# Encoder block with attention, gated linear attention and a mixture of experts: the first block's tokens come by a one-hot product on TensorE instead of a gather from memory, and the first scaling and last sums are reordered

## Chip, cores, metric

One core of one Trainium2 chip. The number told is device microseconds of one execution, the median over runs. The engines are named as the profile names them: PE is TensorE's matmul, PEld its weight load, DVE is VectorE, ACT is ScalarE, POOL is GpSimd, SP is SyncE, whose queue issues most transfers. An engine's name with a q (SPq, POOLq) is its issuing queue.

## What is computed

512 tokens of width 1024, all float32, one layer:

```python
n = rmsnorm(x, norm1_g);  proj = n @ w_in                      # 3104 columns
a = dilated attention(8 heads, 3 branches, relative bias)      # width 512
g = bidirectional gated linear attention(4 heads)              # width 512
x = x + concat([a, g]) @ w_out
h = rmsnorm(x, norm2_g)
logits = h @ router_w + router_b;  top 4 of 32 experts, softmax over the 4
for each block of one expert's tokens:
    hh = h[tokens] @ w1[e] + b1[e]                             # 1024 -> 2048, float32
    act = min(hh[::2], 7) * sigmoid(1.702 * ...) * (clip(hh[1::2], -7, 7) + 1)
    y += gate * (act @ w2[e] + b2[e])                          # 1024 -> 1024
out = rmsnorm(x + y, final_g)
```

## The kernel before

It is written by hand, engine by engine, with semaphores. Three stages follow one another.

**First stage, 0 to 277 us.** SP loads x in four tiles of 128 tokens and then the projection's weights, 2 MB at a time (L409 to L426). For each tile ACT squares and sums (L1057), DVE turns the sum into a mean plus epsilon (`inv_root`, L1260), ACT takes the root (`root`, L1046), DVE inverts it (L1262) and scales the tile (L1267), PE turns it (L554), and DVE or ACT copy it out of PSUM with the norm's weight (`turned_n`, L1271, and L1066). `pre_jobs` (L94) names every filling of a PSUM bank, in order, with the engine that empties it: of the halves of the turned tiles only (2, 1) and (3, 1) are ACT's. When all are out, PE runs the projections (L561, L568) and the two mixers.

**Second stage, 277 to 367 us.** PE multiplies by w_out (`mixed`, L734), half a tile at a time, and between these come, for the tile before, the turning of x (L743), the router's logits (L748), the ranks of the tokens within their experts (`ranks`, L756 and L757) and the table of who sits in which slot (`table`, L767). DVE adds the residual (L1457), picks the four experts (`top4`), turns ranks into one-hot rows (`slotted`, L1491 to L1499) and writes the entries of tokens that do not fit into an expert's 96 slots (`overflowing`). POOL and ACT make the normalised rows HN, and SP stores them to `hn_d` (L457). For the last tile nothing lies between: logits, `top4`, ranks, `slotted`, the total count, the table, its copy T96, its spreading over the partitions (`rep`, L820), and the copies into TABI and TAB (L1545, L1546). Then POOL gathers the first block's 96 rows out of `hn_d` (`gather`, L957) and DVE turns them into XT (`next_tokens`, L1552), in which feature 8p + k lies on partition p. Ahead of `next_tokens` stands DVE's computation of the block maps (L1573 to L1625): which experts have more than 64 tokens, in which order the blocks come, and how many there are. The counts (PAIRS, L1595 to L1599) say how often the loops run; PE, ACT, SP and POOL read them into registers with `value_load`.

**Third stage, from 367 us.** One block of 96 slots (3 groups of 32) after another, 32 experts: PE does `hidden` (L827: W1, 8 MB an expert) and `product` (L834: W2, 4 MB). `expert(i, q, groups)` works on all three groups or, in the second expert of the later pairs, on two. There are two W1 buffers and one for W2; SP reloads a piece when PE has signalled its use (`s_used`, `reload`, L483). The first pieces are loaded in the second stage: `static_w2` at once when the space of w_out is free, the last two of W1's second buffer (L464 and L467) later, since they lie on the router's operands; the first of these waits until the first gather is in (L463).

```python
        for f in range(2):
            static_w2(f, 0)

        sp.wait_ge(s_gath, 16 * NG)
        static_w1(1, 3, 1)
        wait_empty(sp, ("rep",))
        sp.wait_ge(s_pay, NT)
        static_w1(1, 2, 1)
```

Each block's result is added to `sum_d` by an indirect transfer (L1019). The last block's is not: SP loads the sums back (L520), POOL builds one-hot rows OHL (L1031), PE multiplies (L906) into four banks a tile, DVE adds four quarters a tile (`total`, L1697), ACT squares (L1235), and DVE scales (`final_norm`, L1690).

## Time and profile before

| | |
|---|---|
| median of 3 runs | 1380.0 us (1379.21 to 1380.11) |
| the profiled execution | 1385.87 us, span 1384.1 us |
| PE busy | 1266.7 us (92%) |
| DVE / ACT / POOL busy | 537.1 / 221.0 / 338.5 us |
| moved by DMA | 454.15 MB, mean 328 GB/s |
| mean granted TensorE clock | 0.970 of full speed |

The page's times are those of the profiled execution. A busy PE is one with a matmul under way, at whatever clock. Times below are microseconds from the start of the span, nanoseconds where marked.

### The profile page before, as it was taken

The numbers are of one execution on the slowest core, as the hardware profiler recorded it, in microseconds if no ns is written. First come the engines' busy times: TensorE is split into PE (matmuls) and PEld (weight loads), VectorE is DVE, ScalarE is ACT, GpSimd is POOL, SyncE is SP. The second block draws the span as 40 slices with busy tenths as digits, with TensorE's granted clock in tenths as the row PEclk, the third lists the DMA queues.
The fourth block names the chain that finished last, engine by engine and source line by source line (L and its number), as shares of the span: only waits on it lengthen the run. The fifth ranks groups of instructions, "written<-read, shape, count | busy, mean of one in ns | idle before, by whom it ended". The sixth has DMA issues, their size and how long they took to land.

```text
span 1384.1 us, 30020 instructions
## 1 busy us (share of the span) xinstructions
PE 1266.7 (92%) x12121; PEld 650.9 (47%) x12121; DVE 537.1 (39%) x1387; ACT 221.0 (16%) x446; POOL 338.5 (24%) x477
## 2 busy tenths in 40 slices
PE   6999999999599999999998987989898989899995
PEld 3444455655256676454344534343444434346532
DVE  2052353524433333344333444333333333345336
ACT  3052243423100000011000000000100000001102
POOL 2000000013522222223432222232333222222341
PEclk9999999999699999999999999999999999999998
DMA  9310000491799999999999999999999999999995
GB/s 327 114 63 2 27 27 1 161 381 62 304 384 413 410 404 393 401 402 418 414 416 412 413 419 417 417 417 415 415 418 413 413 414 413 416 377 418 394 414 187
DMA packets 62044, 454.15 MB, mean 328 GB/s; under 512 B 15119, under 2 KB 23911, under 8 KB 37436
## 3 DMA queue, kind: packets, MB, share of 16 engines
q1 hardware_dynamic: 40956, 432.18, 75.4%
q0 software_dynamic: 19184, 17.35, 5.7%
q10 hardware_dynamic: 1872, 4.18, 0.8%
q8 instruction: 22, 0.36, 0.1%
q14 instruction: 10, 0.08, 0.0%
HBM read 443.62 MB, written 18.65 MB: 334 GB/s over the span
## 4 chain that ended last, share of the span: by engine, by line
PE 56%; DMA 34%; DVE 3%; issue 2%; POOL 2%; ACT 1%; another core or an unknown queue 1%; POOLq 0%; SPq 0%; DVEq 0%
DMA mem<-in_w 28%; PE bank L827 17%; PE bank L834 16%; PE bank L568 6%; PE bank L561 6%; DMA sum_d<-mem 5%; PE bank L734 4%; PE bank L659 1%; PE bank L610 1%; POOL sum_d L1019 1%; PE bank L697 1%; PE bank L649 1%; POOL mem L957 1%; PE bank L704 1%
## 5 line engine op out<-in xcount | busy, mean ns | idle before, releaser
L827 PE MATMUL bank<-mem 128*32 128x512 f32 x5312 | 591.0, 594 | 14.0 <-DVE mem L1552 10.3
L827 PEld LDWEIGHTS bank<-mem 128*32 128x32 f32 x5312 | 259.9, 110 | 319.4 <-issue 267.3
L834 PE MATMUL bank<-mem 128*32 128x256 f32 x5312 | 339.8, 396 | 72.5 <-DMA mem<-in_w 58.3
L834 PEld LDWEIGHTS bank<-mem 128*32 128x32 f32 x5312 | 206.8, 114 | 202.8 <-DMA mem<-in_w 79.0
L1653 DVE TENSOR_TENSOR mem<-bank,mem 128x512 f32<-128x512 f32 x96 | 64.1, 668 | 412.7 <-PE bank L827 412.7
L1019 POOL DMA_INDIRECT sum_d<-mem x93 | 148.1, 1592 | 16.0 <-issue 16.0
L1221 ACT ACTIVATE mem<-mem 128x256 f32<-128x256 f32 x96 | 43.9, 457 | 607.0 <-DVE mem L1654 607.0
L1007 POOL COPY mem<-mem 128x3 f32 x31 | 6.4, 206 | 539.6 <-issue 539.6
L957 POOL DMA_INDIRECT mem<-hn_d,mem x99 | 103.0, 1040 | 31.8 <-issue 31.6
L1678 DVE TENSOR_TENSOR mem<-bank,mem 128x256 f32<-128x256 f32 x96 | 39.4, 421 | 183.8 <-PE bank L834 107.0
L1227 ACT ACTIVATE mem<-mem 128x256 f32<-128x256 f32 x96 | 47.0, 506 | 318.7 <-DVE mem L1678 258.5
L568 PE MATMUL bank<-mem 128*128 128x512 f32 x192 | 85.6, 599 | 0.0
L561 PE MATMUL bank<-mem 128*128 128x512 f32 x192 | 83.3, 594 | 1.5 <-ACT mem L1066 1.5
L966 POOL TENSOR_TENSOR mem<-mem 128x512 f32<-128x512 f32 x8 | 10.1, 1268 | 223.1 <-DVE mem L1457 223.1
L1663 DVE STREAM_TRANSPOSE mem<-mem 128x256 f32<-128x256 f32 x96 | 62.0, 646 | 3.3
L734 PE MATMUL bank<-mem 128*128 128x512 f32 x128 | 58.0, 598 | 1.2 <-ACT mem L1041 1.2
L561 PEld LDWEIGHTS bank<-mem 128*128 128x128 f32 x192 | 36.2, 190 | 47.9 <-issue 47.0
L568 PEld LDWEIGHTS bank<-mem 128*128 128x128 f32 x192 | 35.5, 190 | 46.7 <-issue 45.5
L933 POOL TENSOR_TENSOR mem<-mem 128x1 f32<-128x1 f32 x130 | 47.9, 368 | 38.5 <-ACT mem L1227 35.5
L1552 DVE STREAM_TRANSPOSE mem<-mem 128x256 f32<-128x256 f32 x99 | 55.3, 609 | 0.0
L1657 DVE SCALAR_TENSOR_TENSOR mem<-mem 128x256 f32<-128x256 f32 x96 | 42.0, 437 | 12.1
L1661 DVE TENSOR_TENSOR mem<-mem 128x256 f32<-128x256 f32 x96 | 41.3, 430 | 3.3
(249 smaller groups left out, 707.0 us busy)
## 6 DMA issues: line engine op xcount, KB each, us to landing
mem<-in_w SPq DMA_DIRECT2D x192, 2048.0 KB
mem<-in_w_in SPq DMA_DIRECT2D x6, 2048.0 KB, 13.1
mem<-in_w_out SPq DMA_DIRECT2D x1, 4096.0 KB, 15.2
mem<-rel_d ACTq DMA_DIRECT2D x8, 448.0 KB, 5.3
mem<-in_x SPq DMA_DIRECT2D x4, 512.0 KB, 5.3
hn_d<-mem SPq DMA_DIRECT2D x4, 512.0 KB, 15.6
sum_d<-mem SPq DMA_DIRECT2D x4, 512.0 KB
mem<-sum_d SPq DMA_DIRECT2D x4, 512.0 KB, 5.0
```

What stands on the lines that cost most here:

```text
L561: m = pe.matmul(b[:, :], w[:, k, c * P:(c + 1) * P], NTt[:, k, :], start=k == 0, stop=k == NK - 1)
L568: m = pe.matmul(b[:, :], NTt[:, k, t * P:(t + 1) * P], w[:, k, :], start=k == 0, stop=k == NK - 1)
L734: m = pe.matmul(b[:, :], MIX[:, k, t * P:(t + 1) * P], WO[:, k, n * 512:(n + 1) * 512], start=k == 0, stop=k == NK - 1)
L827: m = pe.matmul(bank[r][GR * j:GR * (j + 1), :], XT[:, r, k, :], W1[q][:, k, 512 * j:512 * (j + 1)], start=k == 0, stop=k == NK - 1)
L834: m = pe.matmul(bank[3 + r][GR * j:GR * (j + 1), 0:256], ATT[:, r, 2 * f2 + c, :], W2[:, 2 * f2 + c, 256 * j:256 * (j + 1)], start=f2 == 0 ...
L933: pool.tensor_tensor(held[:, 2 + n:3 + n], held[:, 0:1], held[:, 1:2], ALU.add)
L957: pool.indirect_dma_start(out=XG[:, r, :], out_offset=None, in_=quarters, in_offset=bass.IndirectOffsetOnAxis(GI[:, r:r + 1], 0), bounds_c ...
L1019: pool.indirect_dma_start(out=sum_d.ap(), out_offset=bass.IndirectOffsetOnAxis(SI[:, r:r + 1], 0), in_=YN[:, r, :], in_offset=None, bounds ...
L1227: act.activation(YN[:, r, :], YB[:, r, :], ACT.Copy, scale=GTC[:, r:r + 1]).then_inc(s_yn, 1)
L1552: v.transpose(XT[:, r, :, :], XG[:, r, :].rearrange("p (i k) -> p k i", k=NK)).then_inc(s_xt, 1)
L1653: step(v.tensor_tensor(z, bank[r][:, :], B1T, ALU.add))
L1663: v.transpose(ATT[:, r, :, :], ACTV[:, r, :].rearrange("p (i f) -> p f i", f=NF)).then_inc(s_at, 1)
```

## The change

It has five parts.

1. **First scaling.** ACT takes the root straight from its own sum, with epsilon and 1/1024 in the activation (`mean_root`); DVE's step goes. The half (1, 1) of the turned tiles goes from DVE to ACT. DVE's order becomes normalized 0, 1, turned (0,0), normalized 2, turned (0,1), normalized 3, turned (1,0), (2,0), (3,0).
2. **First block's tokens.** In `slotted`, three more DVE operations make OH0, a one-hot row per token with the token's inverse root in the column of its slot if its expert is expert 0. PE multiplies x of each tile (stationary, every eighth column) by OH0: four matmuls of 128x128 by 96 columns for each tile and half, 32 in all, accumulated in two banks. ACT copies them into XT with norm2's weight. The first gather and its turning go; the gather of the second block comes first.
3. **Block maps.** DVE computes the part that the counts need first, and the rest after TABI and TAB.
4. **Loads.** L464's load no longer waits for a gather. The one after it waits also for XT. One small load (G2K, 128 times 32 bytes) stands ahead of w_out's.
5. **Last sums and signals.** The last block's sums for tile 0 start in PSUM with x itself (identity matmuls) and are squared and scaled from there; tile 3 is added in one operation; the order of totals and scalings changes. In two-group experts the second group's signals come from its own last matmul, and the small extra matmul (`also`) signals the third's.

```diff
-    jobs += [(("nT", t, q), "a" if t >= 2 and q else "v") for t in range(NT) for q in range(2)]
+    jobs += [(("nT", t, q), "a" if t and q else "v") for t in range(NT) for q in range(2)]
...
+    OH0 = [view(at + 2 * COLS * (t % NG) + 2 * E + SLOTS * (t // NG), SLOTS) for t in range(NT)]
...
+    WIDE = banks[:, 1024:3072].rearrange("p (j n) -> p j n", j=NJ)[:, :, 0:D // NJ]
...
-    LAST = ((6, 7, 0, 1), (2, 3, 4, 5))
+    LAST = ((2, 3, 4, 5), (6, 7, 0, 1), (6, 7, 0, 1), (2, 3, 4, 5))
...
+        sp.dma_start(G2K, bass.AP(norm2_g.tensor, 0, [[NK, P], [1, NK]])).then_inc(s_g2k, 16)
         sp.dma_start(WO, w_out.rearrange("(k p) n -> p k n", p=P)).then_inc(s_wo, 16)
...
-        sp.wait_ge(s_gath, 16 * NG)
         static_w1(1, 3, 1)
+        sp.wait_ge(s_xt, NG)
         wait_empty(sp, ("rep",))
         sp.wait_ge(s_pay, NT)
         static_w1(1, 2, 1)
...
+        def first_tokens(t, h):
+            b = bank_of(("x0", h))
+            if t == 0:
+                begin(("x0", h))
+            pe.wait_ge(s_oh0, t + 1)
+            for c in range(4):
+                m = pe.matmul(b[:, c * SLOTS:(c + 1) * SLOTS], X[:, t, bass.ds(4 * h + c, P, NK)], OH0[t],
+                              start=t == 0 and c == 0, stop=t == NT - 1, skip_group_check=True)
+            return m
...
         full(("lg", u), logits(b, u, range(4, NK)))
+        first_tokens(0, 0)
+        first_tokens(0, 1)
+        first_tokens(1, 0)
         ranks(u)
...
         full(("total",), pe.matmul(b[:, 0:E], ones, MSEL[:, u, :], start=False, stop=True))
+        first_tokens(1, 1)
+        for t in range(2, u):
+            for h in range(2):
+                first_tokens(t, h)
+        for h in range(2):
+            full(("x0", h), first_tokens(u, h))
         full(("tab",), table(u))
...
-                if r < groups - 1:
+                if r < NG - 1:
                     m.then_inc(s_hf, 1)
             if groups < NG:
-                also().then_inc(s_hf, 1)
+                also().then_inc(s_used, 1)
...
+        pe.wait_ge(s_yl[0], 16)
+        for j in range(NJ):
+            if j:
+                pe.wait_ge(s_yb, 2 * NG * pairs + (NG + j))
+            pe.matmul(bank[LAST[0][j]][:, 0:D // NJ], ident, XF[:, 0, j * (D // NJ):(j + 1) * (D // NJ)],
+                      start=True, stop=False, skip_group_check=True)
...
-        gather(slice(0, 1), 3)
-        pool.wait_ge(s_xt, NG)
-        gather(slice(1, 2), 4)
+        gather(slice(1, 2), 3)
         overflow(3)
...
+        def mean_root(t, done):
+            act.wait_ge(s_sq, done)
+            act.activation(st4[:, t:t + 1], st4[:, t:t + 1], ACT.Sqrt, bias=EPSt, scale=1.0 / D).then_inc(s_sd, 1)
...
+        act.wait_ge(s_g2k, 16)
+        act.wait_ge(s_hst[NT - 2], 16)
+        act.wait_ge(s_hst[NT - 1], 16)
+        for h in range(2):
+            wait_full(act, ("x0", h))
+            for c in range(4):
+                k = 4 * h + c
+                ins = act.activation(XT[:, :, k, :], bank_of(("x0", h))[:, c * SLOTS:(c + 1) * SLOTS].rearrange(
+                    "p (r i) -> p r i", r=NG), ACT.Copy, scale=G2K[:, k:k + 1])
+            if h == 0:
+                emptied_by(ins)
+        ins.then_inc(s_xt, NG)
...
-            v.tensor_scalar(stat, stat, 1.0 / k, EPS, ALU.mult, ALU.add).then_inc(s_var, 1)
...
             link(v.tensor_reduce(RA[:, TOPK * t:TOPK * (t + 1)], OHV, AX.X, ALU.add))
+            link(v.scalar_tensor_tensor(FST, RA[:, TOPK * t:TOPK * (t + 1)], 1.0, OHT[t % 2][:, :, 0], ALU.add, ALU.mult))
+            link(v.tensor_reduce(RK, FST, AX.X, ALU.add))
+            v.tensor_scalar(OH0[t], CF[:, CIO + 1:CIO + 1 + SLOTS], RK, st4[:, t:t + 1],
+                            ALU.is_equal, ALU.mult).then_inc(s_oh0, 1)
...
-        next_tokens(1)
+        v.wait_ge(s_b1, 16)
+        next_b1()
...
         v.wait_ge(s_fg, 16)
-        total(0)
         total(1)
-        for t in range(NT):
+        final_norm(0)
+        total(2)
+        total(3)
+        for t in range(1, NT):
             final_norm(t)
-            if t + 2 < NT:
-                total(t + 2)
```

## Rows read from the trace of the kernel before

**Rows 1.** The page's part 4: share of the chain that ended last

```profile
PE 56%; DMA 34%; DVE 3%; issue 2%; POOL 2%; ACT 1%; another core or an unknown queue 1%; POOLq 0%; SPq 0%; DVEq 0%
```

**Rows 2.** Two experts by windows: length, busy PE to POOL, PEclk, DMA share, GB/s

```profile
402.00:435.00 33.00, 32.77 (x384) 21.75 (x382) 12.34 (x29) 2.92 (x7) 10.12 (x14) 1.00 1.02 411
785.00:817.00 32.00, 27.85 (x301) 11.73 (x297) 12.09 (x29) 2.85 (x6) 9.27 (x13) 0.95 1.02 415
```

**Rows 3.** Timeline of the start: start, length, engine, line, count, idle before, releaser

```profile
2.62 0.48 SPq L413 DMA_DIRECT2D mem<-in_w_in  x1
...
9.52 1.06 ACT L1057 ACTIVATE mem<-mem 128x1024 f32<-128x1024 f32 x1 [0.24 <-DMA mem<-in_x]
...
13.44 0.20 ACT L1046 ACTIVATE mem<-mem 128x1 f32<-128x1 f32 x1 [1.68 <-DVE mem L1260]
...
13.88 0.75 DVE L1267 TENSOR_SCALAR mem<-mem 128x1024 f32<-128x1024 f32 x1
...
14.55 1.88 DVE L1271 TENSOR_TENSOR mem<-bank,mem 128x512 f32<-128x512 f32 x3
...
15.87 1.14 ACT L1066 ACTIVATE mem<-bank,mem 128x128 f32<-128x128 f32 x4 [0.54 <-DVE mem L1271]
...
17.27 7.10 PE L561 MATMUL bank<-mem 128*128 128x512 f32 x16 [1.50 <-ACT mem L1066]
```

**Rows 4.** DMA issues between 2.5 and 2.7 us: count, KB, us to landing

```profile
mem<-in_w_in SPq DMA_DIRECT2D x1, 2048.0 KB, 12.9
```

**Rows 5.** Timeline of the second stage's end, PE, DVE and SP

```profile
347.05 1.31 PE L748 MATMUL bank<-mem 128*128 128x32 f32 x8 [0.94 <-DVE mem L1470]
350.16 0.64 PE L756 MATMUL bank<-mem 128*128 128x32 f32 x2 [1.80 <-DVE mem L1483]
353.31 1.54 PE L767 MATMUL bank<-mem 128*96 128x64 f32 x8 [1.23 <-DVE mem L1499]
...
356.98 0.25 DVE L1546 COPY mem<-bank 128x96 f32<-128x96 f32 x1
...
357.70 0.16 DVE L1512 SCALAR_TENSOR_TENSOR mem<-mem 128x4 f32<-128x4 f32 x1
...
364.61 0.80 SPq L437 DMA_DIRECT2D mem<-in_w  x2
...
367.03 10.61 PE L827 MATMUL bank<-mem 128*32 128x512 f32 x73 [10.27 <-DVE mem L1552]
...
378.03 13.43 SPq L474 DMA_DIRECT2D mem<-in_w  x4
```

**Rows 6.** Windows there, columns as in rows 2

```profile
348.00:350.00 2.00, 0.36 (x2) 0.22 (x2) 1.43 (x7) 1.79 (x3) 1.39 (x3) 0.50 0.46 178
371.00:373.00 2.00, 2.00 (x20) 0.56 (x16) 0.00 (x0) 0.00 (x0) 1.51 (x4) 0.84 1.04 442
362.50:365.00 2.50, 0.00 (x0) 0.00 (x0) 2.23 (x18) 0.00 (x0) 0.00 (x0) 0.50 0.27 95
376.50:379.00 2.50, 2.33 (x21) 0.82 (x19) 0.00 (x0) 0.00 (x0) 0.09 (x1) 1.00 0.12 27
```

**Rows 7.** Timeline: POOL after a register load, PE after a wait and without

```profile
396.90 0.19 POOL L949 TENSOR_TENSOR mem<-mem 128x3 int32<-128x3 int32 x1 [0.67 <-issue]
...
1357.67 5.35 PE L834 MATMUL bank<-mem 128*32 128x256 f32 x64 [2.10 <-DMA mem<-in_w]
```

**Rows 8.** One line each: four DVE sums, strided and not

```profile
L1483 DVE TENSOR_REDUCE mem<-mem x4: 369/372/374, 299.7 to 349.7; 128x32 f32<-128x128 f32 x4
...
L1494 DVE TENSOR_REDUCE mem<-mem x4: 286/286/286, 304.1 to 351.6; 128x4 f32<-128x128 f32 x4
```

**Rows 9.** Timeline of the end, PE and DVE

```profile
1368.16 2.01 PE L906 MATMUL bank<-mem 32*128 32x256 f32 x32 [0.90 <-POOL mem L1031]
1369.47 2.74 DVE L1697 TENSOR_TENSOR mem<-mem,bank 128x256 f32<-128x256 f32 x8 [0.86 <-PE bank L906]
...
1379.68 1.28 DVE L1690 SCALAR_TENSOR_TENSOR mem<-mem 128x1024 f32<-128x1024 f32 x1
```

More of the change, by code:

```diff
@@ L138, in pre_jobs @@
         late += [(("wo", t, 1), "v")]
-    late += [(("xT", NT - 1, 1), "v"), (("lg", NT - 1), "v"), (("rank", NT - 1), "v"), (("total",), "v")]
+    late += [(("xT", NT - 1, 1), "v"), (("lg", NT - 1), "v"), (("rank", NT - 1), "v"), (("total",), "v"),
+             (("x0", 0), "a"), (("x0", 1), "a")]
     for name, e in late:
@@ L220, in encoder_block @@
     JUNK2 = view(take(512), 512)
+    FST, RK, G2K = view(take(TOPK), TOPK), view(take(1), 1), view(take(NK), NK)
     assert at <= o_ks, at
@@ L314, in encoder_block @@
     thr = CF[:, CTH:CTH + THR].unsqueeze(1)
-    bank = [ctx.enter_context(nc.psum_tensor(f"bank{i}", [P, 512], F32)) for i in range(8)]
+    banks = ctx.enter_context(nc.psum_tensor("banks", [P, 8 * 512], F32))
+    bank = [banks[:, 512 * i:512 * (i + 1)] for i in range(8)]
+    WIDE = banks[:, 1024:3072].rearrange("p (j n) -> p j n", j=NJ)[:, :, 0:D // NJ]
     rel_d = nc.dram_tensor("rel_d", [HA, REL], F32)
@@ L905, in _ @@
                 for j in range(NJ):
-                    m = pe.matmul(bank[LAST[t % 2][j]][:, 0:D // NJ], OHL[GR * j:GR * (j + 1), r, t * P:(t + 1) * P],
-                                  YN[GR * j:GR * (j + 1), r, :], start=r == 0, stop=r == NG - 2)
+                    m = pe.matmul(bank[LAST[t][j]][:, 0:D // NJ], OHL[GR * j:GR * (j + 1), r, t * P:(t + 1) * P],
+                                  YN[GR * j:GR * (j + 1), r, :], start=t > 0 and r == 0, stop=r == NG - 2,
+                                  skip_group_check=True)
             m.then_inc(s_add, 1)
@@ L1012, in _ @@
             pool.wait_ge(s_xt, NG * g + 2 * NG)
-            gather(bass.ds(column, 1), g + 5)
+            gather(bass.ds(column, 1), g + 4)
             pool.wait_ge(s_si, g + 1)
@@ L1165, in _ @@
         turned(5, (0, 2))
-        root(NT + 1, st16)
+        root(1, st16)
         turned(6, (0, 2))
@@ L1199, in _ @@
             squares(t, 1)
-            root(NT + 2 + t, st4[:, t:t + 1], EPSt)
+            root(2 + t, st4[:, t:t + 1], EPSt)
             act.wait_ge(s_hx, 2 * t + 2)
@@ new lines, in _ @@
+        v.tensor_scalar(PAIRS[:, N_EARLY:N_EARLY + 1], FULL[0:1, :], float(rest), PNL[0:1, 0:1],
+                        ALU.is_equal, ALU.add).then_inc(s_emap, 1)
+        v.tensor_scalar(PAIRS[:, N_PAIRS:N_PAIRS + 1], FULL[0:1, :], float(rest), PNE[0:1, 0:1],
+                        ALU.is_equal, ALU.add).then_inc(s_emap, 1)
+        wait_full(v, ("rep",))
+        rows = bank_of(("rep",))[:, 0:NG * 2 * E].rearrange("p (g e v) -> p g e v", g=NG, v=2)
+        v.tensor_copy(TABI[:, :, 0:E, 0], rows[:, :, :, 0]).then_inc(s_tabr, 1)
@@ L1583, in _ @@
+        emptied_by(v.tensor_copy(TAB[:, :, 0:E, 1], rows[:, :, :, 1]))
+        overflowing(u)
+        linked(v.tensor_scalar(FULL2, FULL, 2.0, None, ALU.mult),
                v.tensor_scalar(FIRST, FULL, float(rest), None, ALU.add),
@@ L1667, in _ @@
                 swiglu(r)
-            next_tokens(g + 2)
+            v.wait_ge(s_b1, 16 * g + 32)
+            v.wait_ge(s_gath, 16 * NG * g + 16 * NG)
+            for r in range(NG):
+                v.transpose(XT[:, r, :, :], XG[:, r, :].rearrange("p (i k) -> p k i", k=NK)).then_inc(s_xt, 1)
+            next_b1()
             v.wait_ge(s_b2, 16 * g + 32)
```

113 lines of the change are left out of this document (51 added, 62 removed).

## Prediction, made before the changed kernel was run

> **What bounds the kernel now.** I read the chain that ended last first, since the shares of busy time mix three stages. PE holds 56% of it and DMA 34% [rows 1]; in order of time it is PE in the first half of the span and mostly weight loads in the second. The windows say more: already in the expert from 402 to 435 us PE is busy 32.8 of 33 us and the DMA engines are full at 411 GB/s, and in a later one PE has room (27.9 of 32) and the DMA is full at 415 GB/s [rows 2]. An expert's 12 MB of weights, with its tokens fetched and results added, take 32 to 33 us in both. So from the first reload at 378 us [rows 5] the kernel is one long stream of weights, and no part of the change makes the stream shorter. What can be won is its beginning, and the tail behind it. Three places matter: the start, before the first projection; 348 to 378 us, where PE has nothing to do for 10.27 us and the DMA is idle twice; and the last 16 us.
>
> **The start.** In the row of tile 3, ACT has the square done at 10.6 us, but its root starts at 13.44, after 1.68 us of waiting for DVE's step L1260, which stands behind other DVE work [rows 3]. With the root on ACT alone it is there at about 11.0 (10.58, and 0.2 each for reading the sum and for the root). Then DVE counts: when x of tile 3 lands at 9.5 it still has turned (0,0), normalized 2 and turned (0,1) ahead, 0.63 + 0.95 + 0.63 = 2.2 us (1.88/3 a copy; 0.75 and 0.2 for a scaling with its inverse), so that tile 3's scaling starts near 11.9 instead of 13.88. That is 2.0 us less, and PE's first projection would start at 17.27 - 2.0 = 15.3. ACT has one copy more (1.14 us), but ahead of tile 3's, in time that it waits. The next thing that is late is a load: w_in's first 2 MB are issued at 2.62 and land 12.9 us later, at 15.5 [rows 3, 4]. So PE starts at 15.6: **1.6 us** won, and it carries on, for all up to 348 us follows PE, ACT or DVE (bounds: 0.5, if ACT's copies come in its way, and 1.7). The G2K load ahead of w_out costs its issue, 0.48 us as L413's, and PE asks for w_out only after the mixers' last copies; I take 0, and 0.5 for the range. Three more DVE operations in `slotted` for tiles 0 to 2, about 0.2 us each by L1512, lie beside w_out's matmuls: 0.
>
> **The middle**, in times of the profile of before. Logits end at 348.4. PE then waits 1.8 us for ranks at 350.16 [rows 5]. In that gap the change puts 12 of the 32 products, 24 PE instructions (two a float32 matmul). No row has this shape. Nearest are the logits, 8 instructions in 1.31 us, and the ranks, 2 in 0.43 to 0.64, all with 128 columns of weights: 0.107 us at full clock to 0.215 at half. The granted clock is 0.50 at 348 to 350 us, that is 1.2 GHz, and PE had been stopping and starting for 3 us before it fell; after 367.03 it takes 4.6 us of unbroken work until 2.4 GHz is granted (0.84 over 371 to 373) [rows 6]. So the 24 run 4.7 us at half speed (22 of them) and end at 353.3. Ranks and total, 8 instructions, behind them: the rank is there at 353.9, and the total is out at 354.2. Before it was 351.2: the gap filler **costs 2.7 us**.
>
> DVE then does `slotted` with the new three: 2.0 us from rank (351.3) to table operands (353.3) becomes 2.6, to 356.5. PE meanwhile: 24 instructions for (1,1) and tile 2, to 356.8; 16 for tile 3, to 358.6; table, 8 at 0.08 to 0.1, to 359.3 (1.54 before, at half clock); T96 0.25; `rep`, 6, to 360.3; TABI and TAB, as at 356.8 to 357.2, to 360.9. The counts, now ahead of these on DVE, are in by 360.5. ACT's eight copies (0.28 each by L1066 [rows 3]) end 1.4 us after the last product, at 360.1: not last. Last are the two register loads that PE makes after `rep` is emptied and that 5 us of waiting hid before: POOL's load shows 0.67 us [rows 7], so 1.4. PE starts the first expert at **362.3 instead of 367.03: 4.7 us** earlier. Of what was there, the gather, its landing, its turning and DVE's block maps leave the path; the maps still end near 365 on DVE, but SP needs them only for the reload.
>
> The clock: after a wait of 2.1 us at 1355.6 PE took 5.35 us for 64 products of 256 columns, four side by side [rows 7], which at full speed are 16 times 0.22 = 3.5 (L561 takes 0.44 for 512 columns [rows 3]). The wait for the registers is 2 us long, so I take a fall again and 1.8 us lost. Before, 73 products of 512 columns took 10.6 us [rows 5] for 8.0 at full speed: 2.6 lost. That is 0.8 won, 5.5 in all, up to 7.3 if the clock holds.
>
> Against this stands the DMA. It can only be moved up by what it stood idle: 2.5 us at a share of 0.27 and 2.5 at 0.12, 1.8 + 2.2 = 4.0, with the edges about 4.9 [rows 6]. Both gaps go. L437's first load waited until 364.61 for the gather and now follows w2's at once; its second, at about 362, is issued while the first is under way, and together they last to 373; the first reload comes 11 us after PE's start (367.03 to 378.03), at 373.3. Smaller of 5.5 and 4.9: I take **4.8 us**. For POOL, the second block's gather comes ahead of overflow(3) as before, 7 us earlier; nobody waits for it before 387. SP's new wait for XT has only loads behind it and ends before `rep` is emptied.
>
> **The tail.** PE starts on OHL's last row at 1368.16 and DVE ends at 1380.96 [rows 9]; between them DVE does four totals (2.74/2 = 1.37 each) and four scalings (about 1.45), 11.3 us from 1369.47. After: three totals and four scalings, 9.9, from when PE has tiles 0 and 1, which is one identity matmul (0.43) later than before, 1370.7. End at 1380.6: **0.4 us**. Reading four banks at once is unseen here; between 0 and 1.2 us for the range. `also` shifts signals by 0.3 us, where the DMA is the bound: 0.
>
> **Sum.** 1.6 + 4.8 + 0.4 = 6.8 us. The working is made in a profiled execution of 1385.87 us (span 1384.1); I take the difference, not the time, over to the median: 1380.0 - 6.8 = **1373.2 us**.
>
> **A rule that speaks against it.** The stationary operand is every eighth column of x, a step of 32 bytes. The trace has such a step only on DVE: a sum of 128 elements read with a stride takes 0.372 us, without one 0.286 [rows 8]. I keep 0.107 us for PE, since PE's weight loads of 128 columns at either clock just follow the clock. The Trainium skill (SBUF — State Buffer, section "Door 1: The DMA port swizzle") says that full bandwidth needs two accesses to each 16-byte line, so four float32 are the largest free step. By that rule each of the 64 loads would be dearer; the factor is not given.
>
> **Rivals.**
> *Part of the middle is eaten (chance 0.20).* PE's code arrives cold at the loop, register loads take longer than POOL's, or the clock stays low through the 40 later products. For it: everything in 353 to 362 is a chain, and PE has no slack before the loop now. Against: no such stop shows at 277. Middle 1.5: 1376.5 us.
> *The start of the experts doesn't move (0.08).* Then only start and tail count: 1378.0. It would need XT or the counts at 367; nothing above adds up to it.
> *Strided weights cost twice (0.08).* 0.107 more on each of 64: PE is 2.6 us later at ranks and 6.8 later at its first expert, 369.1 instead of 362.3. Middle -2: 1.6 - 2.0 + 0.4 = 0, 1380.0 us. That is where the skill's rule leads, if "dearer" is double.
> *Strided weights cost three times (0.06).* The same place: 13.6 us on the path, 6.9 slower, 1386.9. From 2.4 times on it is slower than before by over 0.2%. For it speaks the DVE pair, which shows that strides are not free; against it that its factor is 1.3.
> *The forecast (0.58).* 1370.5 to 1375.5.
>
> **Chances and range.** A measurement of this kernel tells 0.2%, 2.8 us. Faster by more: forecast, and most of the first rival, 0.76. Within: 0.03 of that rival, the second, the third, 0.18. Slower: 0.06. The range takes the forecast's bounds, the first rival and most of the second: 1370.5 to 1378.3.
>
> **What would show it.** First projection at 15.6, right behind w_in's landing; if at 17, the start failed. PE's ranks at 353.3 less 1.6 with the clock at 0.5; if before 350.5, the filler was free. LDWEIGHTS of the new products as long as others of 128 columns, 0.1 to 0.2 us. First expert at 360.7 (362.3 less 1.6), waiting for a register or `rep`, not XT. No DMA gap between 350 and 380. Last scaling 11.4 us or so after OHL. I am wrong if a weight load in the new line takes 0.3 us, if PE waits for ACT's XT, or if the DMA falls idle elsewhere.

## The result, and the profile after

The changed kernel takes **1383.05 us** (median of 20 runs, 1381.3 to 1385.05) beside 1380.38 us for the kernel before. The ratio is 1.0019, 95% interval 1.0012 to 1.0025: about 2.7 us slower, just under what one measurement tells from no change. Predicted were 1373.2 us and 1370.5 to 1378.3; the prediction was wrong. The profiled execution took 1381.3 us, with a span of 1379.5.

The start did what it should. Timeline of the changed kernel from 10 to 16 us (start, length, engine, line, count, idle before, releaser):

```profile
11.62 0.75 DVE L1314 TENSOR_SCALAR mem<-mem 128x1024 f32<-128x1024 f32 x1
...
15.11 2.84 PE L570 MATMUL banks<-mem 128*128 128x512 f32 x6 [1.59 <-DMA mem<-in_w_in]
```

Tile 3's scaling (L1314) begins at 11.62 instead of 13.88 and the first projection at 15.11 instead of 17.27 [rows 3]; it now waits for w_in's landing and not for ACT. In this execution that is the predicted next thing.

The middle did not. PE's timeline from the last logits to the first expert:

```profile
345.58 1.08 PE L757 MATMUL banks<-mem 128*128 128x32 f32 x8 [0.95 <-DVE mem L1516]
346.50 6.02 PE L775 MATMUL banks<-mem 128*128 128x96 f32 x24
352.31 0.53 PE L765 MATMUL banks<-mem 128*128 128x32 f32 x2
...
353.94 9.81 PE L775 MATMUL banks<-mem 128*128 128x96 f32 x40
363.54 1.44 PE L787 MATMUL banks<-mem 128*96 128x64 f32 x8
365.38 1.51 PE L849 MATMUL banks<-mem 96*128 96x64 f32 x6 [0.41 <-DVE mem L1617]
369.22 11.35 PE L856 MATMUL banks<-mem 128*32 128x512 f32 x88 [2.32 <-issue]
```

L775 is the new product. Its 40 later instructions take 9.6 us, 0.24 us each, where I had 0.107 for an operand of neighbouring columns. The first expert starts at 369.22, later than the 367.03 of before [rows 5], although everything ahead of it came 1.5 us earlier (logits at 345.58 instead of 347.05). From the end of the logits to the first expert it is 22.6 us instead of 18.7. The idle time there is gone: PE is the bound of this stretch. The last wait, 2.32 us "issue", is where the program has PE's two register loads.

The weight load of that line, and for comparison one of the same shape from neighbouring columns (lines from 300 to 380 us, PEld: count, busy us, mean ns, idle before):

```profile
L775 PEld LDWEIGHTS banks<-mem 128*128 128x128 f32 x64 | 15.4, 335 | 0.0
L743 PEld LDWEIGHTS banks<-mem 128*128 128x128 f32 x76 | 13.6, 190 | 12.9 <-issue 12.9
```

335 ns is above the 0.3 us that I had named as the sign of being wrong; the weight loads overlap, so the cost is the spacing, 0.24 us.

Windows of the changed kernel (columns as in rows 2):

```profile
348.00:350.00 2.00, 2.00 (x10) 2.00 (x9) 0.89 (x4) 1.56 (x5) 1.53 (x2) 0.70 1.05 393
360.00:362.00 2.00, 2.00 (x10) 2.00 (x10) 0.00 (x0) 0.04 (x1) 0.00 (x0) 0.50 0.93 393
...
366.00:369.00 3.00, 0.90 (x5) 0.71 (x4) 1.89 (x15) 0.00 (x0) 1.32 (x3) 0.50 0.01 3
371.00:373.00 2.00, 2.00 (x16) 0.49 (x12) 1.76 (x16) 0.00 (x0) 1.82 (x3) 0.58 0.94 389
376.00:378.00 2.00, 2.00 (x24) 0.62 (x20) 0.00 (x0) 0.00 (x0) 0.98 (x1) 1.00 0.33 65
402.00:435.00 33.00, 33.00 (x408) 12.36 (x404) 12.77 (x33) 3.38 (x7) 11.18 (x16) 1.00 1.02 414
785.00:817.00 32.00, 25.52 (x280) 9.67 (x276) 11.72 (x29) 2.74 (x6) 9.26 (x13) 0.89 1.02 417
```

The two experts further on are as before [rows 2]: the stream of weights is as fast as it was. The DMA gap at 362 to 365 [rows 6] is closed, but two new ones are there, 366 to 369 and 376 to 378. And the granted clock falls while PE is busy, 0.70 over 348 to 350, and is at 0.50, 1.2 GHz, at 360 and up to the first expert, though from 346.5 to 366.9 PE stopped once, for 0.4 us; over 371 to 373 it is still 0.58.

SP's timeline names the loads behind the two gaps:

```profile
349.75 19.27 SPq L446 DMA_DIRECT2D mem<-in_w  x2
376.93 0.35 SPq L483 DMA_DIRECT2D mem<-in_w  x1
```

L446's first load (W1's last piece but one) is issued at 349.75, behind w2's, as the change wants. Its second is issued only at the end of that group, at 368.70, after a wait of 18.3 us. SP's waits, and ACT's copies of the second half of XT:

```profile
SPq L475 <- DVE mem L1566: 18.3, 1, 18.3
...
363.79 1.03 ACT L1254 ACTIVATE mem<-banks,mem 128x96 f32<-128x96 f32 x4 [0.79 <-PE banks L775]
```

The program has three waits there: XT (the new one), `rep` emptied, and `s_pay`. XT was complete at 364.82. L1566 is the last of DVE's entries of the last tile's tokens (`overflowing`), which signals `s_pay`; it stands behind TABI and TAB on DVE and ended at 368.60. So it is a wait that was there before, and it is late because the table is: the long products hold it up.

The first reload (L483) needs PE's first uses of the first expert, and comes at 376.93; before it was 378.03 [rows 5].

The tail, DVE's timeline:

```profile
1366.87 1.41 DVE L1758 TENSOR_TENSOR mem<-mem,banks 128x256 f32<-128x256 f32 x4 [2.88 <-PE banks L943]
...
1371.01 1.22 DVE L1754 TENSOR_TENSOR mem<-mem,banks 128x1024 f32<-128x1024 f32 x1
...
1375.13 1.28 DVE L1747 SCALAR_TENSOR_TENSOR mem<-mem 128x1024 f32<-128x1024 f32 x1
```

From PE's last L863, at 1358.95, to DVE's end at 1376.41 it is 17.46 us. Before, from L834's 1363.29 (of the same trace as rows 9) to 1380.96, it was 17.67. The tail won 0.2 us. The addition that reads four banks at once takes 1.22 us, where four separate ones take 1.41.

### The profile page after: what moved, and what is told of

It is laid out like the page before. It is cut to its first block, busy times and chain, and to the rows that moved or that the text cites. A ratio compares the mean times of both kernels' runs of the same rounds, so it can differ in the third digit from the quotient of the medians.

```text
span 1379.5 us, 30137 instructions
## 1 busy us (share of the span) xinstructions
PE 1257.6 (91%) x12193; PEld 542.7 (39%) x12193; DVE 532.2 (39%) x1384; ACT 223.4 (16%) x458; POOL 335.1 (24%) x472
## 4 chain that ended last, share of the span: by engine, by line
PE 58%; DMA 37%; DVE 3%; issue 1%; ACT 1%; SPq 0%; DVEq 0%
DMA mem<-in_w 37%; PE banks L863 17%; PE banks L856 16%; PE banks L577 6%; PE banks L570 6%; PE banks L743 4%; PE banks L775 1%; PE banks L668 1%; PE banks L619 1%; DMA mem<-in_w_in 1%; PE banks L706 1%; PE banks L658 1%; PE banks L713 1%; PE banks L757 0%; PE banks L641 0%
## 5 line engine op out<-in xcount | busy, mean ns | idle before, releaser
L856 PE MATMUL banks<-mem 128*32 128x512 f32 x5312 | 579.9, 595 | 5.9 <-DMA mem<-in_w 3.6
L863 PE MATMUL banks<-mem 128*32 128x256 f32 x5312 | 316.7, 398 | 91.3 <-DMA mem<-in_w 84.2
L856 PEld LDWEIGHTS banks<-mem 128*32 128x32 f32 x5312 | 169.3, 110 | 393.5 <-issue 384.5
L863 PEld LDWEIGHTS banks<-mem 128*32 128x32 f32 x5312 | 171.1, 115 | 238.2 <-DMA mem<-in_w 106.9
L1700 DVE TENSOR_TENSOR mem<-banks,mem 128x512 f32<-128x512 f32 x96 | 63.6, 663 | 411.6 <-PE banks L856 411.6
L1056 POOL DMA_INDIRECT sum_d<-mem x93 | 148.1, 1592 | 17.6 <-issue 17.6
L1731 DVE TENSOR_TENSOR mem<-banks,mem 128x256 f32<-128x256 f32 x96 | 39.4, 421 | 176.7 <-PE banks L863 176.7
L995 POOL DMA_INDIRECT mem<-hn_d,mem x96 | 99.9, 1041 | 31.1 <-issue 31.1
L577 PE MATMUL banks<-mem 128*128 128x512 f32 x192 | 85.6, 599 | 0.0
L570 PE MATMUL banks<-mem 128*128 128x512 f32 x192 | 83.4, 594 | 1.6 <-DMA mem<-in_w_in 1.6
L971 POOL TENSOR_TENSOR mem<-mem 128x1 f32<-128x1 f32 x129 | 50.9, 394 | 35.1 <-ACT mem L1279 31.9
L743 PE MATMUL banks<-mem 128*128 128x512 f32 x128 | 58.0, 598 | 1.2 <-ACT mem L1078 1.2
L570 PEld LDWEIGHTS banks<-mem 128*128 128x128 f32 x192 | 36.2, 190 | 48.0 <-issue 46.2
L577 PEld LDWEIGHTS banks<-mem 128*128 128x128 f32 x192 | 35.5, 190 | 46.7 <-issue 45.5
```

The source lines that it names most:

```text
L570: m = pe.matmul(b[:, :], w[:, k, c * P:(c + 1) * P], NTt[:, k, :], start=k == 0, stop=k == NK - 1)
L577: m = pe.matmul(b[:, :], NTt[:, k, t * P:(t + 1) * P], w[:, k, :], start=k == 0, stop=k == NK - 1)
L743: m = pe.matmul(b[:, :], MIX[:, k, t * P:(t + 1) * P], WO[:, k, n * 512:(n + 1) * 512], start=k == 0, stop=k == NK - 1)
L856: m = pe.matmul(bank[r][GR * j:GR * (j + 1), :], XT[:, r, k, :], W1[q][:, k, 512 * j:512 * (j + 1)], start=k == 0, stop=k == NK - 1)
L863: m = pe.matmul(bank[3 + r][GR * j:GR * (j + 1), 0:256], ATT[:, r, 2 * f2 + c, :], W2[:, 2 * f2 + c, 256 * j:256 * (j + 1)], start=f2 == 0 ...
L971: pool.tensor_tensor(held[:, 2 + n:3 + n], held[:, 0:1], held[:, 1:2], ALU.add)
```

## The experiments

**Theories.** S: the products' stationary operand is every eighth column, and its weight load costs 0.24 us instead of 0.107; this holds up PE and, through it, the last early load and the first reloads. Rivals: the two-group signals (part 5) let the loads of the later experts come late; the products ahead of the ranks are the cost and the rest is free; the start's gain was never there. The runs of one group below were made on one chip with the kernel before beside them; two_step, listed with the third, had a group of its own. The groups differ: in the result's, the second and the third the kernel before takes 1380.4 to 1380.5 us, in the first 1387.3 and in two_step's 1386.4. So only ratios are compared across groups.

### First group: the same kernel again, the start alone, two parts undone

**before_again**, no edit.

> The kernel before, unchanged, for a second profile. Its first profiled execution took 1385.87 us, 5.5 us above its median, and moved 394 to 411 GB/s between 432 and 592 us, where the changed one moved 410 to 418. If that was this one execution's own trouble, the new profile shows 413 or more there, a time near 1380.4 and a last weight wait that ends near 1358; then the changed kernel's stream is about 4 us longer than the typical one of before, and that needs a cause. If it is a trait of the kernel before, the rates repeat near 400.

Measured: ratio 1.0 (0.9991 to 1.001), profiled execution 1384.2 us. The second trace of the kernel before was worth more than I thought. Its windows and SP's timeline:

```profile
363.00:364.00 1.00, 0.00 (x0) 0.00 (x0) 0.86 (x8) 0.00 (x0) 0.00 (x0) 0.50 0.01 0
...
376.50:379.00 2.50, 2.50 (x32) 0.67 (x27) 0.00 (x0) 0.00 (x0) 0.00 (x0) 1.00 0.79 295
```

```profile
373.77 5.48 SPq L474 DMA_DIRECT2D mem<-in_w  x2
```

The first gap is there, the second is not (share 0.79 where rows 6 have 0.12), and the first reload comes at 373.77, not at 378.03. The gap of 376.5 to 379 on which 2.2 us of my DMA term rested belonged to that one execution: start_only and start_tail, which have the same middle, don't show it either (shares 0.99 and 0.97). The other half of the expectation came out as a level: from 432 to 592 us before_again moves 395 to 408 GB/s, close to the 394 to 411 of the first trace. It is not the kernel's trait, though, for start_tail below, with the same middle and in another group, moves 411 to 415 there.

**start_only**: the kernel before with part 1 alone.

```diff
+            mean_root(t, t + 1)
...
-            v.tensor_scalar(stat, stat, 1.0 / k, EPS, ALU.mult, ALU.add).then_inc(s_var, 1)
```

> Kernel before with the first scaling of the change alone. In the changed kernel's trace the first projection starts at 15.11 instead of 17.27 us. Theory A (the start is won for good, the whole weight stream shifts): 2.1 us faster, about 1378.3. Theory B (a win at the start is lost later, because the stream is bound by something that does not shift): 0 to 0.5 us faster.

Measured: ratio 0.9988 (0.9978 to 0.9998), 1.7 us faster; the first projection at 15.69 instead of before_again's 16.62. It is less than theory A's 2.1 us, and the interval is only just clear of 1.

**old_signals**: the changed kernel with the signals of two-group experts as before.

```diff
-                if r < NG - 1:
+                if r < groups - 1:
...
-                also().then_inc(s_used, 1)
+                also().then_inc(s_hf, 1)
```

> Changed kernel with the two-group experts' signals as before (the third group's clamp and the last W1 reload released by the second group's own last matmul, the second group's by the small extra one). Theory S (the later release of a W1 or W2 reload by 0.33 us in each two-group expert lengthens the stream): 3 to 4 us faster than the changed kernel, about 1379.5. Rival (the weight queue always has a backlog): within 0.5 us of the changed kernel, 1383.

Measured: ratio 1.0025 (1.0014 to 1.0036). The loss stays: the signals are not its cause.

**ranks_first**: the changed kernel with no products ahead of the ranks; all 32 come after the total.

```diff
-        first_tokens(0, 0)
-        first_tokens(0, 1)
-        first_tokens(1, 0)
         ranks(u)
...
-        first_tokens(1, 1)
-        for t in range(2, u):
+        for t in range(u):
```

> Changed kernel with none of the 32 products ahead of the last ranks; all come after the total count. PE then takes the ranks at about 348.7 instead of 352.3 us. Theory C (PE is the bound between 346 and 365, all 64 instructions at 1.2 GHz, 0.24 us each): the 24 move behind, PE's idle time of 2 us before the ranks comes back, and the table ends 2 us later: 1 to 2 us slower than the changed kernel. Rival (the DVE chain behind the ranks is the bound, or the clock rises since PE has had its pause elsewhere): 1 to 3 us faster.

Measured: ratio 1.0044 (1.0027 to 1.0061). PE's timeline:

```profile
351.22 15.55 PE L775 MATMUL banks<-mem 128*128 128x96 f32 x64
...
372.26 2.79 PE L852 MATMUL banks<-mem 128*32 128x512 f32 x12 [2.35 <-issue]
```

64 products in a row, 0.24 us each, and the first expert 2.1 us later than in old_signals (370.12), which is the nearest run of this group; by their medians it is 2.0 us slower. Filling the gap with 24 of them was right; with all 64 behind the total it is worse still. That points at the products' own length.

### Second group: the length of the products

**after_again**, the changed kernel.

> The changed kernel, unchanged, beside the next three and the kernel before on one chip. The profiled executions so far came from chips that differ by some 7 us. Theory C (the 64 product instructions at 0.24 us hold PE's first expert back): 2.5 to 3.5 us slower than before, first expert at 369 to 370 us, DMA idle near 366 to 369.

Measured: 1383.36 us, ratio 1.0021 (1.0011 to 1.003); 40 products in 9.83 us and the first expert at 370.06, as in the first trace.

**contiguous**: the stationary operand is 128 neighbouring columns. The first block's sums are then of other features than W1's rows, so its result is another one; every operation and transfer is of the same size.

```diff
-                m = pe.matmul(b[:, c * SLOTS:(c + 1) * SLOTS], X[:, t, bass.ds(4 * h + c, P, NK)], OH0[t],
+                m = pe.matmul(b[:, c * SLOTS:(c + 1) * SLOTS], X[:, t, (4 * h + c) * P:(4 * h + c + 1) * P], OH0[t],
```

> Changed kernel with the stationary operand of the products read contiguously (128 neighbouring columns, so the first block's tokens are other sums than the reference's) instead of every eighth column. Rival St (the 32-byte step makes the weight loads dear): LDWEIGHTS below 0.336 us and a product instruction at 0.1 to 0.2 instead of 0.24, 2 us or more faster than the changed kernel. Theory C (the price is the clock's): 0.21 to 0.24 each, within 1.5 us of it.

Measured: **1376.4 us**, ratio 0.9972 (0.9959 to 0.9984), 7.0 us below after_again on the same chip, by one operand's address step. PE's timeline and the windows of the same stretch:

```profile
347.35 5.41 PE L775 MATMUL banks<-mem 128*128 128x96 f32 x24
...
354.18 7.57 PE L775 MATMUL banks<-mem 128*128 128x96 f32 x40
...
360.58 1.17 PE L775 MATMUL banks<-mem 128*128 128x96 f32 x9
361.58 0.82 PE L787 MATMUL banks<-mem 128*96 128x64 f32 x8
...
366.00 12.20 PE L856 MATMUL banks<-mem 128*32 128x512 f32 x96 [2.35 <-issue]
```

```profile
358.00:360.00 2.00, 2.00 (x11) 2.00 (x11) 0.00 (x0) 0.00 (x0) 0.00 (x0) 0.50 0.94 401
360.00:362.00 2.00, 2.00 (x21) 2.00 (x19) 0.00 (x0) 1.03 (x5) 0.00 (x0) 0.94 1.06 451
...
366.00:369.00 3.00, 3.00 (x20) 0.88 (x24) 2.76 (x21) 0.00 (x0) 2.31 (x3) 0.68 0.88 291
```

At 1.2 GHz the instructions follow each other by 0.213 us, start to start in the trace, where the strided ones take 0.24: 12% more. The third row is the end of the second, in a narrower window, when the clock is 2.4 GHz: 9 instructions from 360.58 to 361.58, 0.111 us each. Against 0.24 that is 2.2 times, and my 0.107 was a little low even for neighbours. And here the clock is granted at 360 us, while in the changed kernel it stayed at 0.50 beyond 369. The gap of 366 to 369 is nearly closed (0.88 instead of 0.01). This kernel has W1's old order, so the order of that load is not what wins.

**half_products**: two products of four, so that half of the first block's features are left out (ACT copies the other half twice), with the 32-byte step kept.

```diff
-            for c in range(4):
+            for c in range(2):
...
-                ins = act.activation(XT[:, :, k, :], bank_of(("x0", h))[:, c * SLOTS:(c + 1) * SLOTS].rearrange(
+                ins = act.activation(XT[:, :, k, :], bank_of(("x0", h))[:, (c % 2) * SLOTS:(c % 2 + 1) * SLOTS].rearrange(
```

> Changed kernel with two of the four products for each tile and half (32 PE instructions instead of 64, half of the first block's features are left out and the other half is copied twice). Theory C: the products stand on the path, 12 before the ranks, of which 1.8 us were idle anyway, and 20 after them: PE's first expert 1 + 4.8 = 5 to 6 us earlier, 4 to 6 us faster than the changed kernel, 2 to 3 faster than before. Rival (DVE's chain or the signals bound it): under 2 us faster.

Measured: 1376.34 us, ratio 0.9969 (0.9956 to 0.9981). PE's timeline:

```profile
362.63 7.74 PE L856 MATMUL banks<-mem 128*32 128x512 f32 x44 [2.35 <-issue]
```

The first expert is 7.4 us earlier than after_again's 370.06, more than the 5 to 6 expected, with 32 instructions fewer: 0.23 us each, on the path. Their number counts as their length does. And it is 3.4 us earlier than in contiguous (366.00), while the time is the same (1376.34 and 1376.40 us). An earlier start on PE alone won nothing more there, as the prediction has it when it takes the smaller of what PE and the DMA allow.

**products_early**: the products of tiles 0 and 1 between w_out's matmuls, where PE is warm, with two PSUM banks held for them, so that five instead of seven are shared by the other work.

```diff
+                if t - 1 < 2:
+                    for h in range(2):
+                        first_tokens(t - 1, h)
...
-        first_tokens(0, 0)
-        first_tokens(0, 1)
-        first_tokens(1, 0)
+        first_tokens(2, 0)
         ranks(u)
...
```

> Changed kernel with the products of tiles 0 and 1 placed behind the table of the same tile, among w_out's matmuls where PE is granted 2.4 GHz; tile 2's first half fills the gap before the ranks; the other banks are shared by five instead of seven. Theory C (same work, cheaper at the high clock): 32 instructions cost 3.4 us more up to the ranks and 7.7 less later, the first expert about 3.5 us earlier than in the changed kernel, and the time 2.5 to 4 us below it, at or just under the kernel before. Rival: if the clock is not the cause, 0.24 us each there too, and no gain.

Measured: ratio 1.0043 (1.0028 to 1.0057), slower. PE's timeline, and its window with the clock:

```profile
305.70 4.00 PE L778 MATMUL banks<-mem 128*128 128x96 f32 x16
309.53 1.91 PE L746 MATMUL banks<-mem 128*128 128x512 f32 x4
```

```profile
306.00:309.00 3.00, 3.00 (x14) 3.00 (x14) 0.09 (x1) 0.00 (x0) 0.00 (x0) 1.00 0.46 190
```

16 in 3.83 us, 0.239 each, at a granted clock of 1.00. That is the cleanest price: **the strided load isn't faster at 2.4 GHz than at 1.2**. And it is paid in full there. Up to the logits PE is the bound: the last logits (L760) start at 353.81, where after_again has them at 346.39. That is 7.4 us later, for 32 products of 0.24 us (7.7). The first expert stays at 370.11. To move strided products to where the clock is high gains nothing, since the clock doesn't help them. Why the median is 2.4 us above after_again's its trace doesn't show: the profiled execution was the fastest of five, with 1383.36 us as long as after_again's 1383.2.

### Third group: a repair, the step's size, and the rest of the change

If an expert's rows of W1 are loaded in another order, the columns of x may be neighbours and the sum is the reference's. Only the first block of the first expert uses these products, and that expert's W1 is loaded once, by its own code.

**repaired**:

```diff
-            sp.dma_start(W1[q][:, 2 * k:2 * k + 2, :],
-                         w1[e].rearrange("(p k) n -> p k n", k=NK)[:, 2 * k:2 * k + 2, :]).then_inc(s_w1[q][k], 16)
+            rows = w1[e].rearrange("(p k) n -> p k n", k=NK) if q else w1[e].rearrange("(k p) n -> p k n", p=P)
+            sp.dma_start(W1[q][:, 2 * k:2 * k + 2, :], rows[:, 2 * k:2 * k + 2, :]).then_inc(s_w1[q][k], 16)
...
-                m = pe.matmul(b[:, c * SLOTS:(c + 1) * SLOTS], X[:, t, bass.ds(4 * h + c, P, NK)], OH0[t],
+                m = pe.matmul(b[:, c * SLOTS:(c + 1) * SLOTS], X[:, t, (4 * h + c) * P:(4 * h + c + 1) * P], OH0[t],
...
-                    "p (r i) -> p r i", r=NG), ACT.Copy, scale=G2K[:, k:k + 1])
+                    "p (r i) -> p r i", r=NG), ACT.Copy, scale=VT[:, V2 + k:V2 + k + 1])
```

> The changed kernel with the products' stationary operand as 128 neighbouring columns of x (4-byte step), and, to match it, the first expert's W1 loaded with row 128k+p on partition p instead of 8p+k, so that everything that the reference asks for is computed; the G2K load goes, since norm2's weight is already on the chip in that order. Theory (the 32-byte step of the weight loads is what the change paid for): as the kernel 'contiguous', products 0.107 us each at 2.4 GHz and 0.215 at 1.2 GHz, 24 of them in about 5.4 us and 40 in about 7.6 us against 6.0 and 9.8; first expert on PE 4 us earlier than in the changed kernel, near 366; first reload near 374; time 6 to 7 us below the changed kernel's, ratio to the kernel before 0.996 to 0.998. Rival (what 'contiguous' won came from its other numbers or from its other first block): time as the changed kernel's, ratio 1.002. Second rival (the weights' other order makes the early loads of W1 slower): DMA busier before 350 us, first expert waits for W1, over 370.

Measured: **1375.89 us**, ratio 0.9973 (0.9961 to 0.9984). By the ratios it beats the kernel before by 3.7 us and the changed one (1.0021 in after_again) by 6.6. PE's and SP's timelines:

```profile
353.59 7.30 PE L774 MATMUL banks<-mem 128*128 128x96 f32 x40
...
365.15 13.06 PE L855 MATMUL banks<-mem 128*32 128x512 f32 x104 [2.35 <-issue]
```

```profile
351.02 13.91 SPq L446 DMA_DIRECT2D mem<-in_w  x2
372.83 5.05 SPq L482 DMA_DIRECT2D mem<-in_w  x2
```

The last early load goes out at about 365 instead of 369, and the first reload at 372.83 instead of 376.93.

**start_tail**: the kernel before with parts 1 and 5, that is the changed kernel without its middle.

```diff
+            mean_root(t, t + 1)
...
-    LAST = ((6, 7, 0, 1), (2, 3, 4, 5))
+    LAST = ((2, 3, 4, 5), (6, 7, 0, 1), (6, 7, 0, 1), (2, 3, 4, 5))
```

> The kernel before with parts 1 and 5 of the change alone (first scaling; last sums and signals), without the first block's products, the block maps' other order and the loads. Theory (start won 1.7 us and the tail 0.2 to 0.5, and all of the loss lies in the middle): time 1.9 to 2.2 us below the kernel before, ratio 0.9984 to 0.9986; from the last weights' products of PE to the end 17.3 to 17.5 us instead of 17.67. Rival (tail or signals cost something): not below start_only's ratio of 0.9988, or above 1.

Measured: 1379.63 us, ratio 0.9994 (0.9985 to 1.0003): 0.7 us faster, less than the 1.9 to 2.2 expected, with the expectation's edge just inside the interval. From the last L838 (1356.59) to the end (1374.06) it is 17.47 us, as in the changed kernel. So of start_only's 1.7 us a part did not show here; start and tail together are worth between 0.7 and 1.7 us as medians, and I can't say closer.

What the middle does to the stream shows in wide windows (columns as in rows 2). First the changed kernel, then start_tail, then repaired:

```profile
340.00:360.00 20.00, 19.05 (x92) 17.32 (x90) 9.14 (x42) 6.63 (x12) 6.14 (x8) 0.72 0.63 250
360.00:380.00 20.00, 17.27 (x118) 9.13 (x121) 8.21 (x58) 2.07 (x8) 8.64 (x12) 0.68 0.72 274
380.00:400.00 20.00, 20.00 (x272) 8.14 (x268) 10.44 (x24) 1.86 (x4) 4.04 (x9) 1.00 0.98 369
400.00:1200.00 800.00, 716.90 (x8496) 277.28 (x8492) 296.63 (x730) 71.38 (x152) 238.71 (x333) 0.96 1.02 415
```

```profile
340.00:360.00 20.00, 11.28 (x58) 8.66 (x56) 11.34 (x63) 7.20 (x13) 8.91 (x13) 0.72 0.60 236
360.00:380.00 20.00, 13.91 (x116) 3.88 (x120) 6.57 (x37) 0.00 (x0) 8.33 (x11) 0.77 0.87 345
380.00:400.00 20.00, 20.00 (x288) 8.70 (x284) 11.84 (x29) 2.87 (x6) 6.37 (x12) 1.00 1.01 376
```

```profile
340.00:360.00 20.00, 19.05 (x105) 16.79 (x104) 10.32 (x45) 7.52 (x13) 6.15 (x8) 0.74 0.57 223
360.00:380.00 20.00, 17.25 (x146) 6.72 (x149) 8.20 (x58) 1.96 (x8) 10.09 (x14) 0.91 0.96 380
380.00:400.00 20.00, 20.00 (x288) 9.48 (x284) 11.84 (x29) 2.88 (x6) 5.99 (x11) 1.00 1.00 377
```

The last column is GB/s. Over 340 to 400 us they move 20 x (250 + 274 + 369) = 17.9 MB, 19.1 MB and 19.6 MB, and from 400 to 1200 us all three go at 414 or 415 GB/s. At that rate 19.1 less 17.9 MB is 3.1 us, and 19.6 less 19.1 is 1.1 us. By the ratios the changed kernel (after_again, 1.0021) is 3.7 us behind start_tail (0.9994), and repaired (0.9973) 2.9 us ahead of it. So the loss of the changed middle is in the stream (after_again moves 17.6 MB, which makes it 3.8 us), and of the repaired one's win about a third is seen there; each ratio is uncertain by some 1.5 us, and the rest, 1.8 us, stays open.

**four_step** and **two_step**: every fourth column (16 bytes) and every second (8 bytes), each with the first expert's W1 and G2K in the matching order.

```diff
-                m = pe.matmul(b[:, c * SLOTS:(c + 1) * SLOTS], X[:, t, bass.ds(4 * h + c, P, NK)], OH0[t],
+                m = pe.matmul(b[:, c * SLOTS:(c + 1) * SLOTS], X[:, t, bass.ds(512 * h + c, P, 4)], OH0[t],
...
```

> The changed kernel with the stationary operand as every fourth column of x (16-byte step; feature 512h + 4p + c), and, to match it, the first expert's W1 and G2K loaded in that order, so that everything that the reference asks for is computed. It asks how the weight load's time depends on the step. Theory A (The Trainium skill, page 'SBUF - State Buffer', section 'Door 1: The DMA port swizzle', by which four fp32 are the largest free step; its text is weighed here against a weight load): products as with neighbouring columns, 0.107 us at 2.4 GHz and 0.215 at 1.2 GHz, 40 of them in about 7.6 us, time as 'repaired' within 1 us, ratio 0.996 to 0.998. Theory B (every step above 4 bytes costs alike): 0.24 us each at either clock, 24 in 6.0 us and 40 in 9.8, ratio 1.002. Theory C (the cost grows with the step): between 0.15 and 0.2 us each at 2.4 GHz, the time between the two.

Measured: 1383.48 us, ratio 1.002 (1.0011 to 1.0029), theory B:

```profile
354.24 9.61 PE L778 MATMUL banks<-mem 128*128 128x96 f32 x40
...
369.30 9.21 PE L859 MATMUL banks<-mem 128*32 128x512 f32 x68 [2.31 <-issue]
```

The 40 take 0.235 us each, from 354.24 to the table at 363.64. It too has its own order of W1's rows, and that gives it nothing, so the win of repaired comes from the products' step and not from a new order of the loads.

```diff
-                m = pe.matmul(b[:, c * SLOTS:(c + 1) * SLOTS], X[:, t, bass.ds(4 * h + c, P, NK)], OH0[t],
+                m = pe.matmul(b[:, c * SLOTS:(c + 1) * SLOTS], X[:, t, bass.ds(512 * h + 256 * (c // 2) + c % 2, P, 2)], OH0[t],
...
```

> The changed kernel with the stationary operand as every second column of x (8-byte step; feature 256g + 2p + c), and, to match it, the first expert's W1 and G2K loaded in that order, so that everything that the reference asks for is computed. Known by now: a 4-byte step costs 0.107 us at 2.4 GHz and 0.215 at 1.2 GHz, steps of 16 and 32 bytes 0.24 us at either. Theory A (what counts is how often a 16-byte line is read in a row: twice here): free, 24 products in about 5.4 us or less and 40 in 7.3 to 7.6 us, first expert 365 to 366, ratio 0.996 to 0.998. Theory B (any step but 4 bytes is dear alike): 24 in 6.0 us and 40 in 9.7 us, first expert 369 to 370, ratio 1.002. Theory C (between, by the number of lines read): 40 products in 7.6 us as long as the clock is at 1.2 GHz and over 0.12 us each at 2.4 GHz.

Measured: 1383.33 us where the kernel before takes 1386.42, ratio 0.9975 (0.9963 to 0.9988), as good as repaired within the intervals. Its twelve runs spread from 1379.0 to 1387.0 us, and the profiled one took 1386.74.

```profile
347.22 5.42 PE L778 MATMUL banks<-mem 128*128 128x96 f32 x24
...
361.04 0.99 PE L778 MATMUL banks<-mem 128*128 128x96 f32 x7
```

Free at 1.2 GHz, where its 24 take 5.42 us as contiguous's 5.41. The last seven ran at 2.4 GHz: from 361.04 to the table's first instruction at 361.86 they take 0.117 us each, where contiguous has 0.111. So it is nearly free there too. Theory B is out; C's "over 0.12" wasn't reached, and A's "free" is off by 5%.

## Why the prediction was wrong, step by step

**The bound** was read rightly: the time follows when the stream of weights gets going, and the stream itself didn't change. That an earlier PE wins only what the DMA allows is borne out by half_products beside contiguous.

**The start** (1.6 us) was right in mechanism: first projection at 15.11 and, in after_again, 15.93, right behind w_in's landing, where I had 15.6. As time, 1.7 us in start_only; with the tail, 0.7 us in start_tail. The size is less sure than I wrote. The 17.27 from which it was worked out was late even for the kernel before (16.62 in before_again), and in six of the twelve traces with the new start, start_tail's and repaired's among them (both 16.39), the first projection waits for a copy of ACT's and not for w_in.

**The step that failed** is "I keep 0.107 us for PE". It cost 0.24 us at either clock, 2.2 times what I took. I had the right doubt and gave it 0.08 and 0.06: the rival "strided weights cost twice" put the first expert at 369.1, less the start's 1.6, and it came at 369.22, still later. The page of the Trainium skill that I set against the trace, "SBUF — State Buffer", section "Door 1: The DMA port swizzle", says that full bandwidth needs two accesses to each 16-byte line; a 32-byte step has one, and the traces agree in direction (at 2.4 GHz 0.239 us to 0.111). What kept me from it was DVE's pair [rows 8], whose factor is 1.3: one engine's factor said nothing of the other's, 2.2. The same passage of the Trainium skill gives four float32 as the largest free step; four_step's 0.235 us speaks against that for weight loads, two_step's 8 bytes (0.117) are in line with the two accesses.

**The clock was the second failed step**, and hung on the first only in part. From 354.2 us on I let PE run at full clock because after 367.03 it had been granted after 4.6 us of work [rows 6]. It was still at 0.50 at 358 to 360 even in contiguous, whose PE was busy without a break since 346.07, and in the changed kernel it stayed low up to the first expert and beyond, to 372.7. The three kernels with cheap loads (contiguous, repaired, two_step) were granted 2.4 GHz between 359 and 361 us, while the products ran, and none with dear ones before its first expert; what decides it no run shows. From the logits' end to the first expert I had 13.9 us, it was 22.6. By pieces, measured less predicted: up to the ranks 0.75, ranks and total 0.7, the 40 products 5.2, table and T96 0.9, `rep` and registers 1.1. In contiguous the same stretch is 18.5 us (347.54 to 366.00). So 4.1 of the 8.7 us go with the step, by the load itself and by the clock that stayed low with it, and 4.6 would have been there anyway. Of these 3.0 are the 40 products, most of which ran at 1.2 GHz in contiguous too. Another 0.7 is a misreading: I gave ranks and total 0.9 us, but the eight instructions take some 1.7 in the trace of before as well (350.16 to about 351.9); the 351.2 from which I counted is the end of the ranks. The rest is in table and `rep`, and in the registers, 2.35 us for 2.0.

**Without the stride the first expert would still hardly have come earlier on PE**: 18.5 us after the logits, against 18.7 before. The predicted 4.7 us by PE were not to be had with these products. What contiguous and repaired win is the DMA's: the gap of 362 to 365 is closed, since the early loads no longer wait for a gather. That is read from the traces; no run has parts 3 and 4 alone.

**The DMA term** (4.8 us in the sum, though the smaller of 5.5 and 4.9 is 4.9) took two gaps; before_again shows that the second, 2.2 us, is not typical of the kernel before. The right bound was 2.5 us or so, an estimate from the first gap and its edges. With the start's 1.6 and the tail, a kernel with free products comes to 1.6 + 2.5 + 0.2 = 4.3 us. Repaired measured 3.7, between 2.2 and 5.4 by its interval; with the start's size open, that the two are so close is in part luck.

**The late load.** I had "SP's new wait for XT" down as harmless, and so it was: XT came at 364.82, before `rep` was emptied (367.36, the end of DVE's copy into TAB). But the load behind it waits 18.3 us in the changed kernel, until DVE's last entries at 368.60, and leaves the DMA idle from 366 to 369. In my sum it would have been issued at 362 beside a running load; it hung on the same 0.107 us, through the table.

**The tail** (0.4 us) was 0.2. `also` and the signals at 0 were right: old_signals loses what the changed kernel loses.

**The range** left out both rivals on the strided load, 1380.0 for twice and 1386.9 for three times, with 0.14 between them. The truth, 2.2 times my 0.107 and 1383.05 us, lies between the two. For a price that no row of its shape showed, that was too little. By their own terms the chances of faster and within are 0.75 and 0.19, not 0.76 and 0.18; that changes nothing.

## What to carry to other kernels

A stationary operand read with a step must be priced from a row of its own form, or by both bounds: here 128 float32 columns at a step of 16 or 32 bytes took 0.23 to 0.24 us at either clock, and neighbours 0.111 at 2.4 GHz and 0.213 at 1.2, so the step ate all that the fast clock gives. If the step only serves a layout, turn the other operand's load instead: a transfer that is there anyway took the other row order for nothing, and that turned 1.0021 into 0.9973. And read two executions of the kernel before, before a gap of 2 us goes into a sum.

## What the runs showed that I had not expected

- The strided load's spacing is the same at both clocks: 0.239 us at a granted clock of 1.00 (products_early), 0.240 at 0.50 (changed kernel). With neighbouring columns it is 0.111 and 0.213 (contiguous).
- PE busy without a break isn't enough to be granted 2.4 GHz soon. Products of neighbouring columns had it at 360 us, 12.7 us after they began; strided ones didn't have it from 350 to 369 us, and in half_products not from 356 to 358 us either (0.50).
- Where PE makes its two register loads with nothing to hide them, it stands still for 2.31 to 2.35 us in all kernels with the change, by an estimate 1.2 us each, where POOL's load after other work shows 0.67 [rows 7].
- The same kernel took 6 to 7 us more in two groups of runs than in the others. Whether that is the chip is open: the record has the number 3 for the chip of the first group (1387.3 us) and of the third (1380.4). The traces show it in the stream of weights: from 432 to 592 us before_again moves 399 GB/s on average and start_tail, of the third group, 414, which over 160 us makes 5.6 us. By its time and its rates the trace from which the prediction was worked out is one of the slower kind.
